# Gate vectors of the second mixer: from full-precision broadcasts of four rows to high and low parts broadcast by single-pass products

## The reference, cut to what matters

```python
b = jnp.cumsum(fc, axis=-1)                       # log forget gates within a chunk
log_inter = b + m[..., None]
m_q = jnp.maximum(log_inter, jnp.max(log_intra, axis=-1))
w_intra = jnp.exp(log_intra - m_q[..., None]) * (q @ k.T)
w_inter = jnp.exp(log_inter - m_q)                # one value for each query
h = num / jnp.maximum(jnp.abs(den), jnp.exp(-m_q))[..., None]
w_key = jnp.exp(log_key - m_new[..., None])       # one value for each key
decay = jnp.exp(b_last + m - m_new)               # one value for each chunk
```

## Time and profile before

| | |
|---|---|
| runs before | 2808.14, 2813.56, 2816.01 us |
| profiled execution, its own time | 2812.45 us |
| its span | 2810.6 us |
| mean granted TensorE clock | 0.967 of full |
| PE busy | 2660.5 us, 95% of the span |
| DVE busy | 1387.9 us, 49% |
| ACT busy | 1005.6 us, 36% |
| POOL busy | 819.3 us, 29% |
| mLSTM, head 0 to the outputs of head 3 | 1936.4 to 2222.0 us |

### The profile page before, as it was taken

The page is one execution under the profiler, slowest core; times in us unless marked ns, Lnnn a source line. Parts: engine busy times, 40 slices in busy tenths (PEclk is TensorE's granted clock), DMA queues, the critical chain, the costliest instruction groups (busy, mean ns, idle before and its releaser), DMA issues.

```text
span 2810.6 us, 36029 instructions
## 1 busy us (share of the span) xinstructions
PE 2660.5 (95%) x14132; PEld 2197.5 (78%) x14132; DVE 1387.9 (49%) x1841; ACT 1005.6 (36%) x1694; POOL 819.3 (29%) x645
## 2 busy tenths in 40 slices
PE   7988999999999889999999799988999999999998
PEld 6966788888798667888887688867877688788887
DVE  2738754553327586554533445547444533433332
ACT  5458722222244585222222444452223200222222
POOL 5567623333236466234343010120000012100000
PEclk8999999999999999999999899989998999999999
DMA  5320035554432100265555121211111134233332
GB/s 129 92 57 7 11 88 135 136 150 130 125 93 87 49 1 20 79 157 135 142 136 141 32 61 46 61 31 30 46 46 46 46 105 122 59 92 103 84 89 82
DMA packets 396745, 230.51 MB, mean 82 GB/s; under 512 B 9772, under 2 KB 392876, under 8 KB 396576
## 3 DMA queue, kind: packets, MB, share of 16 engines
q1 hardware_dynamic: 394608, 226.19, 29.5%
q0 software_dynamic: 1968, 2.01, 0.8%
HBM read 226.07 MB, written 2.10 MB: 81 GB/s over the span
## 4 chain that ended last, share of the span: by engine, by line
PE 75%; DVE 9%; ACT 8%; DMA 5%; issue 2%; POOL 0%; SPq 0%; DVEq 0%; ACTq 0%; POOLq 0%
PE ps L845 64%; PE scores L845 8%; DMA raws<-in_w_down 4%; PE ps L990 1%; ACT wH L1840 1%; DVE R L2192 1%; DVE wL L2402 1%; DMA ring<-in_w_in 1%; DVE ring_parts L2455 1%; DVE R L2533 0%; ACT spare L1702 0%; ACT R L1707 0%; ACT U L1679 0%; ACT U L1702 0%; ACT R L1679 0%
## 5 line engine op out<-in xcount | busy, mean ns | idle before, releaser
L845 PE MATMUL ps<-xH,wH 128*128 128x512 f32 x1000 | 395.5, 395 | 6.5 <-DVE xL L2377 4.3
L845 PE MATMUL ps<-xL,wH 128*128 128x512 f32 x1000 | 391.2, 391 | 0.0
L845 PE MATMUL ps<-xH,wL 128*128 128x512 f32 x1000 | 390.6, 391 | 0.0
L1840 ACT ACTIVATE wH<-raws 128x2048 fp32r<-128x2048 f32 (+1 forms) x114 | 192.9, 1693 | 493.3 <-PE ps L845 349.3
L845 PE MATMUL ps<-ring_parts,U_parts 128*128 128x256 f32 (+2 forms) x2000 | 340.1, 297 | 22.1 <-DVE ring_parts L2259 6.2
L2402 DVE TENSOR_TENSOR wL<-raws,wH 128x2048 fp32r<-128x2048 f32 (+1 forms) x114 | 232.1, 2036 | 246.5 <-ACT wH L1840 245.2
L845 PEld LDWEIGHTS ps<-ring_parts,U_parts 128*128 128x128 f32 x2000 | 297.6, 202 | 35.0 <-issue 27.3
L736 POOL TENSOR_TENSOR spare<-spare,cvec 128x1024 f32<-128x1024 f32 x64 | 122.8, 1919 | 441.2 <-DMA spare<-in_w_ada 441.2
L811 POOL CAST ring_parts<-ring 128x2048 fp32r<-128x2048 f32 x34 | 66.7, 1961 | 621.2 <-DMA ring<-in_w_in 542.1
L845 PE MATMUL ps<-R 128*64 128x128 f32 (+4 forms) x1528 | 220.0, 317 | 27.0 <-DVE R_parts L2213 7.0
L845 PE MATMUL ps<-U_parts,ring_parts 128*128 128x512 f32 (+2 forms) x768 | 226.7, 384 | 0.4 <-DVE ring_parts L2455 0.4
(11 more groups left out here) (450 smaller groups left out, 4772.9 us busy)
## 6 DMA issues: line engine op xcount, KB each, us to landing
raws<-in_w_gate_up SPq DMA_DIRECT2D x88, 512.0 KB, 5.7
ring<-in_w_in SPq DMA_DIRECT2D x34, 1024.0 KB, 5.8
spare<-in_w_ada SPq DMA_DIRECT2D x64, 512.0 KB, 4.0
raws<-in_w_down SPq DMA_DIRECT2D x32, 704.0 KB, 6.0
raws<-in_w_ffn_in SPq DMA_DIRECT2D x44, 512.0 KB, 5.2
ring<-in_w_in SPq DMA_DIRECT2D x26, 512.0 KB, 5.3
raws<-in_w_ffn_out SPq DMA_DIRECT2D x16, 704.0 KB, 4.7
ring<-in_w_o SPq DMA_DIRECT2D x12, 448.0 KB, 3.8
```

The costliest lines, as they stand in the source:

```text
L845: return nc.tensor.matmul(o, a, b, start=first, stop=last)
L1840: ap.do(f(wH[:, g % 2, 0:n], raws[:, g % 2, 0:n], ACT.Copy), wh_ready)
```

## The change

The rows are held on all 128 partitions instead of 4. The gates are taken out by a selector `fourth` (16 by 128, built by GpSimd from `ident`) that puts the four heads on partitions 0 to 3 and again on 32 to 35 (`LOW_AT`). DVE's and ScalarE's work on rows then runs over 128 partitions at the same length. What is to be broadcast stands in two tiles, X (w_inter, the 6 decays and w_key, 1286 columns) and E (512), and in rT (A, 512). ScalarE rounds each to float32r parts (`rX`, `rE`, `rA`) and, on partitions 32 to 35 alone, GpSimd then replaces the rounded value by the rest (`rows_low`). `pick`, now 128 partitions of float32r and computed on GpSimd, has a one at partition h and one at 32 + h, so that one product in float32r adds high and low part.

With that, `mrow` loses its exponentials (the decays are in X), DVE's copy into `rA` is gone, one exponential takes the place of three, the 6 decays and the 256 context keys are one product of 262 columns, and E is one product of 512 columns instead of four of 128. The eight transposes of exp(-m) move behind the state products of head 0, direction 0, and `emc_ready` is gone.

```diff
-        pick = C[0:NH2, 256:768].rearrange("p (a b) -> p a b", a=NH2)
+        LOW_AT = 32
+        pick = C_parts[:, 256:768].rearrange("p (a b) -> p a b", a=NH2)
...
+            def rows_low(d):
+                pool.wait_ge(rows_high, d + 1)
+                low = slice(LOW_AT, LOW_AT + NH2)
+                for row, part in ((X[d], rX[d]), (E[d], rE[d]), (rT[d][:, 256:768], rA[d])):
+                    pg.do(nc.gpsimd.tensor_tensor(part[low, :], row[low, :], part[low, :].bitcast(F32), ALU.subtract))
+                pg.also(rows_split)
+
             for j in range(SECOND.index(("gate", NH2)), len(SECOND)):
+                if j in ROWS_BEFORE:
+                    rows_low(ROWS_BEFORE.index(j))
                 round_piece(j)
...
-                job(db, lambda b: b[:, :], [(sel, rWK[d][:, 256:768])])
+                job(db, lambda b: b[:, :], [(sel, rX[d][:, 774:1286])])
                 some(between, 3)
-                bank = db.fill(pe)
-                mm(bank[:, 0:256], sel, rWK[d][:, 0:256], True, True)
-                mm(bank[:, 256:262], sel, mrow[:, d, 3, :], True, True).then_inc(d_full, 1)
+                job(db, lambda b: b[:, 0:262], [(sel, rX[d][:, 512:774])])
                 some(between, 2)
-                job(db, lambda b: b[:, :], [(sel, rWI[d][:, :])])
+                job(db, lambda b: b[:, :], [(sel, rX[d][:, 0:512])])
                 run(between)
                 bank = db.fill(pe)
+                mm(bank[:, :], sel, rE[d], True, False)
                 for j in range(TT):
-                    mm(bank[:, j * P:(j + 1) * P], sel, rE[d][:, j * P:(j + 1) * P], True, False)
-                    ins = mm(bank[:, j * P:(j + 1) * P], rA[d][:, j * P:(j + 1) * P], sel, False, True)
+                    ins = mm(bank[:, j * P:(j + 1) * P], rA[d][:, j * P:(j + 1) * P], sel, False, j == TT - 1)
...
             for d in range(2):
                 ap.more(rows_ready)
-                ap.do(f(rM[d], rM[d], ACT.Exp, scale=-1.0), max_exp)
-                ap.do(f(rWK[d], rWK[d], ACT.Exp))
-                ap.do(f(rWI[d], rWI[d], ACT.Exp))
-                ap.do(f(mrow[:, d, 3, :], mrow[:, d, 2, :], ACT.Exp), rows_exp)
+                ap.do(f(maxima[d], rM[d][0:NH2, 256:768], ACT.Exp, scale=-1.0), max_exp)
+                ap.do(f(X[d], X[d], ACT.Exp))
+                for row, part in ((X[d], rX[d]), (E[d], rE[d]), (rT[d][:, 256:768], rA[d])):
+                    if d == 1:
+                        act.wait_ge(rows_split, 1)
+                    ap.do(f(part, row, ACT.Copy))
+                ap.also(rows_high)
...
+                if d == 1:
+                    dve.wait_ge(rows_split, 1)
...
-                vp.do(v.tensor_copy(rA[d], rT[:, 256:768]))
```

More of the change, by code:

```diff
@@ L92, in build @@
         xT = sb("xT", [P, KT, S])
-        C = sb("C", [P, 2944])
+        with ExitStack() as tables_at:
+            C = tables_at.enter_context(nc.sbuf_tensor("C", [P, 2944], F32))
+        C_parts = sb("C_parts", [P, 2944], mybir.dt.float32r)
         ident = sb("ident", [P, P])
@@ L562, in second_dmas @@
             return [(dst, cols(w, o[n] + h * DV, o[n] + (h + 1) * DV))]
+        ROWS_BEFORE = [SECOND.index(name_h) for name_h in (("gate", NH2 + 1), ("qk", NH2 + 2))]
         read_second = [None] * len(SECOND)
@@ L1398, in _, with maxima_by_token @@
             run(nxt("k", 1))
-            pp.more(max_exp, 2)
-            bank = db.fill(pe)
-            for d in range(2):
-                for j in range(TT):
-                    o = (d * TT + j) * NH2
-                    ins = nc.tensor.transpose(bank[:, o:o + NH2], rM[d][:, 256 + j * P:256 + (j + 1) * P], ident[0:NH2, 0:NH2])
-            ins.then_inc(d_full, 1)
+            def maxima_by_token():
+                pp.more(max_exp, 2)
+                bank = db.fill(pe)
+                for d in range(2):
+                    for j in range(TT):
+                        o = (d * TT + j) * NH2
+                        ins = nc.tensor.transpose(bank[:, o:o + NH2], maxima[d][:, j * P:(j + 1) * P], ident[0:NH2, 0:NH2])
+                ins.then_inc(d_full, 1)
             def mlstm_scan(h, d, nxt):
@@ L1436, in mlstm_scan @@
                 pe.wait_ge(a_free, transposed)
+                if h < 2 and d == 0:
+                    pe.wait_ge(ones_set, h + 1)
                 between = nxt("v", 3) if d == 0 else nxt("gate", 0)
@@ L1440, in mlstm_scan @@
                     some(between, 2)
+                if h == 0 and d == 0:
+                    maxima_by_token()
                 pp.more(sc_ready)
@@ L2634, in _ @@
             second_low("v", NH2 + 1)
-            bank = db.take(dve)
-            vp.do(v.tensor_copy(emc[:, :, :, :].rearrange("p a b c -> p (a b c)"), bank[:, 0:2 * TT * NH2]), d_free)
-            vp.do(v.memset(head(1)[2][:, :, DV:DV + 1], 1.0), emc_ready)
+            vp.do(v.memset(head(1)[2][:, :, DV:DV + 1], 1.0), ones_set)
             def mlstm_outputs(h, d):
@@ L2667, in mlstm_outputs @@
                 states(block_order(d), STm, DV + 1, lambda c: dec[:, d, c:c + 1])
+                if h == 0 and d == 0:
+                    bank = db.take(dve)
+                    vp.do(v.tensor_copy(emc[:, :, :, :].rearrange("p a b c -> p (a b c)"), bank[:, 0:2 * TT * NH2]), d_free)
                 for t in range(TT):
@@ L2762, in constants @@
     bias = np.stack([np.where(fwd, 0, -1e30), np.where(bwd, 0, -1e30)], 1).astype(f)
-    pick = np.zeros((NH2, NH2, P), f)
-    for h in range(NH2):
-        pick[h, h] = 1
     return {
```

86 lines of the change are left out of this document (46 added, 40 removed).

## The result

The changed kernel took 2784.03 us in the median of four executions (2780.52 to 2786.76), the kernel before beside it 2812.71: a ratio of 0.989, 95% interval 0.987 to 0.9909. The forecast was 2784. Run again later, beside other executions of the kernel before, it gave 2784.50 and 0.9897 (0.9881 to 0.9912).

A forecast was written before the change was run, and what follows sets the result against it. The prediction took TensorE (PE), busy for 95% of the span, as the bound, the mLSTM included. From 2812.45 us, −17.4 (products), +2.3 (front), +0.6 (transposes) and −13.6 (clock) made −28.1: 2784 us, range 2768 to 2803.

The forecast's parts named there:

- The products: Broadcast products of the mLSTM: 3.35 us saved per group, 26.8 for eight at most, 17.4 after waits.
- The front: Start of head 0: GpSimd's subtractions take DVE's time, the w_inter broadcast comes 4.2 us later, net +2.3 us.
- PE's start at 1935.5: Head 0: PE would wait for the weight piece alone and could start at 1935.5 us, not 1936.4.
- The transposes: Eight small transposes, now behind head 0, direction 0's state products where PE is busy: up to 1.01 us, taken as +0.6.
- The clock: Half-clock stretches in the mLSTM go with full-height products: −13.6 us, with 11.6 more not counted.
- some 5 us of them in 9: Claim that some 5 us of products using 4 of 128 rows, in a stretch of 9, precede the clock's falls.
- The sum: All terms for the kernel together: −17.4 + 2.3 + 0.6 − 13.6 = −28.1 us.
- Rival 1: The mLSTM's clock stays as it is: −14.5 us, 2798; chance 0.22.
- Rival 2: Front: no contention from GpSimd's subtractions, as they touch 4 partitions only: −34.4 us, 2778; chance 0.13.
- Rival 4: Float32r products of 128 columns with new weights cost 0.35 us each, a group saves 2.2: 2790; chance 0.04.
- Rival 5: Slower: GpSimd's six subtractions and DVE wait for each other at the front: +7.7 us, 2820; chance 0.05.
- Rival 3: Waits replace products: DVE sets the pace in the first directions' groups: −6 us, 2806; chance 0.08.

The follow-up runs named there:

- the early piece: Changed kernel with DVE's subtraction of head 1's first piece of values ahead of the second direction's rows instead of behind them: 2781.32 us (0.9889).

## Why the prediction was right, point by point

The causes of the terms were right. Their sizes were less so: the clock gave more than was counted, the front cost more, and the rest of the program took some back, so part of the hit is luck.

- **The products: 17.4 us, ceiling 26.8.** The prices were right (0.62 for E with A against 0.89 allowed, 0.12 for 262 columns). What was lost to waits too: 1.53 us at head 1 (1.2 said), and head 3 kept its ScalarE wait, 4.71 instead of 2.75. The reason given was incomplete: the old price was not one of plain float32 alone. A group costs 4.67 us 4 high in float32, 2.95 at full height in float32, 2.0 in a single pass at 4 high and 1.3 with both. So the height is worth 1.7 us of the old price or 0.7 of the new one, depending on which is changed first. The rows of before couldn't show it, since every selector product there was 4 high.
- **The front: +2.3 us.** The w_inter broadcast was 4.8 us later than before, corrected for the 3.0 by which PE finished the projections later (4.2 said: 1954.46 − 3.0 − 1946.70). DVE lost 3.6 + 3.8 = 7.4 us to the subtractions (7.6 said), and taking them out shortened PE's two waits by 7.2. Two errors met in the 7.6: GpSimd's six instructions took 5.35 + 5.36 = 10.7 us in the trace and not 8.66, and DVE lost 0.69 of that and not 0.88. Behind it, (0,0)'s E with A at half clock cost 1.17. At the first transposes of the keys the term stood at 1957.76 − 3.0 − 1950.99 = +3.8, 1.5 more than said: 0.6 from the broadcast, 0.4 since the two products behind it saved 0.72 + 0.81 and not 1.9, and 0.5 since the projections between them ran at half clock. One statement on the way was wrong: PE's start at 1935.5. It waits for a subtraction that DVE has queued behind the rows, and so started at 1943.96 − 3.0 = 1941.0. That cost nothing more, because the second wait shrank by it; the early piece shows this (12.60 + 2.53 became 2.75 + 10.49).
- **The transposes: +0.6.** 0.65, from 1966.69 to the next product less its wait.
- **The clock: −13.6, with 11.6 not counted.** The mechanism was right, and the size was between: half of the length of stretches with PE busy was 25.3 us in the eight of before and 5.0 in the three that are left in the changed kernel (head 0, direction 0, behind PE's wait of 2.53 us, and two in head 3, the last from 2197 us on, just behind the stage). That is 20.3 of the 25.2. The term that was mis-sized was head 2, direction 0, with 5.1, which I left out since PE also waits there; the stretch went anyway in the first profile, and was 3.4 instead of 10.2 us long in the second. One reading was wrong: "some 5 us of them in 9" did not stand ahead of every fall. The three long stretches begin at 1972.6, 2102.0 and 2129.5, ahead of E and A, with 2.6 to 2.8 us of the group done. What PE gained this way it partly gave back in waits.
- **The sum** of the stage was −28.1 and it is −35.0 and −31.3 in two profiles; the medians differ by 28.7. The rest of the program took back 3.1 us in the first profile. That the forecast met the median within a microsecond is therefore in part luck.
- **The rivals.** Rival 1 (the clock stays) is refuted by the granted clock of 0.97. The rule that the Trainium skill, "TensorE: Matmul & The Clock Gate", "What's actually happening", gives (the gate goes by how busy PE has been) does not tell these cases apart as long as busy is read as busy time: 11.00 of 11.00 us at 1.2 GHz, 4 high, against 10.84 of 11.00 at 2.4 GHz, 128 high. Ahead of a fall it is no better: 5.42 of 6.00 us busy, 4 high, and the clock fell; 4.73 of 6.00, 128 high, and it stayed. Read as busy time, the rule disagrees with these traces; they show that the height of the products counts, and not in which measure. Rival 2 (no contention) is refuted: subtractions on 4 partitions blocked DVE for 7.4 us. Rival 4 (dear products of 128 columns) is refuted: the four of A start within 1976.56 − 1976.17 = 0.39 us. Its arithmetic was off too, since at 0.35 each a group would still save 2.6 us and not 2.2. Rival 5 (a convoy) didn't come: DVE lost seven tenths of what GpSimd spent, once.
- Rival 3, waits in place of products, was real as a part: PE's idle time in the stage rose by 10.8 us, with the front's second wait the largest. That is why 51.6 us less of busy PE gave 40.8.

## What to carry to other kernels

Beside making a small broadcast or selector product cheaper by its number format, look at its height. With 512 columns it cost 0.1 to 0.2 us more over 4 partitions than over 128 in a single pass, and 0.5 to 0.6 more over 4 or 36 in float32; and where such products stood close together, the clock fell to half behind most groups. Full height cost nothing on the engines that make the rows (a scan of 4x768 took 1.75 us on DVE and one of 128x768 1.76; on ScalarE an exponential of 4x768 took 0.85 and the activation of a 128x768 tile 0.84). The selector is zero in the unused partitions, so their rows add nothing whatever finite values stand there. It is a change of shape, not of precision: the changed kernel with its products left in float32 but at full height stands 17 us under the kernel before, and the one with single-pass products 4 high 19 us.

Price a subtraction on GpSimd beside dense DVE work as time of DVE: here seven tenths of what GpSimd took, 3.7 us a trio, where DVE does it itself in 2.9. GpSimd's time went with the columns here: 1286 on 4 partitions took 2.51, 1024 on 128 took 1.92. And where one engine paces another, moving its work only moves the wait until the work leaves the stretch, and then whatever is queued behind it in the next stretch wants a look.

## What the runs showed of the hardware

- In a single pass a low product hardly costs more in itself; the passage from full-height products to low ones and back does. From start to start of the w_inter broadcast 4x512 took 0.43 us and 128x512 took 0.23, and four in a row took 1.13 (4 high) and 0.92 (128 high): 0.2 more, once and not four times. For float32 (1.02 to 1.05 against 0.45 to 0.53) no run tells the passage from the product.
- A tenth of a microsecond decides which engine pays. Where DVE's instruction was recorded 0.10 us ahead of GpSimd's cast, the cast was the longer one (2.41 us); where it was 0.03 ahead, DVE was (2.46). The same two meet in head 2 in all fourteen traces. In four of them DVE is recorded 0.08 to 0.11 us ahead, and the cast paid (2.39 to 2.43); in the other ten, the kernel before among them, DVE is between 0.04 ahead and 0.10 behind, and DVE paid (2.33 to 2.48, with the cast at 1.89 to 1.90). The Trainium skill, "SBUF — State Buffer", "SBUF: two separate sides", says that whichever starts first gets the port pair and the other fully blocks. The first case agrees (GpSimd lost 0.5, most of what DVE had left of its 0.75); in the second the loser is recorded as the first, so the start in the records is not the moment at which the pair is taken.
- The lock also stretched a DVE instruction with one tensor input: the scaling beside the second trio took 1.40 us for 0.55. It is of the faster kind: from 256 to 512 columns it takes 0.13 us more (0.42 and 0.55), those with two inputs 0.26 (0.49 and 0.75).
